# Down projection of a gated FFN: rounds 1 and 2 as seven block products instead of eight, with block sums on GpSimd

## What is computed

```
h2 = rmsnorm(x, norm2_g)
up, new_conv_f = causal_dwconv(h2 @ w_up, state_ffn_conv, conv_f_w, conv_f_b)   # 1024 -> 6144
gf, vf = split(up, 2)
x = x + (gelu(gf) * vf) @ w_down                                                # 3072 -> 1024
```

## Time and profile before

| | us |
|---|---|
| median of 3 runs | 1171.17 |
| lowest, highest | 1170.28, 1171.51 |
| span of the profiled execution, first to last instruction | 1168.8 |
| its own time | not listed apart from the span |
| PE busy | 1161.8 (99%) |
| DVE, ACT, POOL busy | 655.9 (56%), 455.9 (39%), 167.4 (14%) |

### The profile page before, as it was taken

The page is one execution under the profiler, slowest core; times in us unless marked ns, Lnnn a source line. Parts: engine busy times, 40 slices in busy tenths (PEclk is TensorE's granted clock), DMA queues, the critical chain, the costliest instruction groups (busy, mean ns, idle before and its releaser), DMA issues.

```text
span 1168.8 us, 21548 instructions
## 1 busy us (share of the span) xinstructions
PE 1161.8 (99%) x8959; PEld 1131.1 (97%) x8959; DVE 655.9 (56%) x1336; ACT 455.9 (39%) x719; POOL 167.4 (14%) x261
## 2 busy tenths in 40 slices
PE   8999999999999999999999999999999999999998
PEld 6999999999999999999999999999999999999998
DVE  7553544624522365756545559878347884378741
ACT  7444444434423367676443443222212222122221
POOL 2374153252330000000100120000000000000000
PEclk9999999999999999999999999999999999999999
DMA  8476255354431222221353223232322323232332
GB/s 242 144 212 174 79 140 150 97 149 124 132 93 55 73 77 74 85 73 56 123 143 90 73 73 90 72 90 77 91 80 83 88 73 95 72 90 72 90 99 61
DMA packets 183492, 118.50 MB, mean 101 GB/s; under 512 B 7114, under 2 KB 175694, under 8 KB 183418
## 3 DMA queue, kind: packets, MB, share of 16 engines
q1 hardware_dynamic: 172272, 89.44, 27.0%
q0 software_dynamic: 11056, 28.01, 8.6%
q10 hardware_dynamic: 90, 0.04, 0.0%
HBM read 107.43 MB, written 8.45 MB: 99 GB/s over the span
## 4 chain that ended last, share of the span: by engine, by line
PE 98%; DMA 1%; DVE 0%; ACT 0%; SPq 0%; issue 0%
PE ps L664 66%; PE ps L643 20%; PE ps L968 2%; PE ps L733 1%; PE ps L720 1%; PE ps L883 1%; PE ps L776 1%; PE ps L801 1%; PE ps L797 1%; PE ps L745 1%; PE ps L807 1%; DMA w_raw<-in_w_in 1%; PE ps L761 1%; PE ps L764 1%; PE ps L765 0%; PE ps L955 0%
## 5 line engine op out<-in xcount | busy, mean ns | idle before, releaser
L664 PE MATMUL ps<-h,w_s 128*128 128x288 f32 x3840 | 517.5, 296 | 0.0
L664 PEld LDWEIGHTS ps<-h,w_s 128*128 128x128 f32 x3840 | 512.6, 189 | 3.9 <-issue 3.9
L1453 DVE TENSOR_TENSOR w_s<-w_raw,w_s 128x1024 fp32r<-128x1024 f32 (+1 forms) x160 | 194.0, 1212 | 220.4 <-ACT w_s L1054 220.3
L1054 ACT ACTIVATE w_s<-w_raw 128x1024 fp32r<-128x1024 f32 (+1 forms) x160 | 166.3, 1039 | 334.4 <-PE ps L664 329.8
L643 PE MATMUL ps<-w_s,h 128*128 128x384 f32 x1152 | 217.5, 341 | 1.7 <-DVE w_s L1459 0.7
L643 PEld LDWEIGHTS ps<-w_s,h 128*128 128x128 f32 x1152 | 198.7, 188 | 3.7 <-DVE h L1480 1.2
L664 PE MATMUL ps<-g_hi,w_s 128*128 128x288 f32 x672 | 119.1, 297 | 0.0
L664 PEld LDWEIGHTS ps<-g_hi,w_s 128*128 128x128 f32 x672 | 99.4, 189 | 0.0
L664 PE MATMUL ps<-g_lo,w_s 128*128 128x288 f32 x336 | 71.9, 296 | 0.0
L605 POOL DMA_DIRECT2D out<-f_row x6 | 3.4, 567 | 415.1 <-ACT f_row L1403 415.1
L664 PEld LDWEIGHTS ps<-g_lo,w_s 128*128 128x128 f32 x336 | 54.1, 189 | 0.0
(11 more groups left out here) (309 smaller groups left out, 1429.3 us busy)
## 6 DMA issues: line engine op xcount, KB each, us to landing
w_raw<-in_w_in SPq DMA_DIRECT2D x65, 512.0 KB, 3.9
w_raw<-in_w_up SPq DMA_DIRECT2D x48, 512.0 KB, 3.9
w_raw<-in_w_down SPq DMA_DIRECT2D x24, 512.0 KB, 3.8
kc<-in_cache_k_g POOLq DMA_DIRECT2D x48, 128.0 KB, 3.2
vc<-in_cache_v_g POOLq DMA_DIRECT2D x12, 512.0 KB, 6.3
w_raw<-in_w_out SPq DMA_DIRECT2D x8, 512.0 KB, 3.8
w_raw<-in_w_br_a SPq DMA_DIRECT2D x7, 512.0 KB, 3.9
x_tok<-in_x_prompt SPq DMA_DIRECT2D x4, 512.0 KB, 8.3
```

What stands on the lines that cost most here:

```text
L664: last = mm(pu[u % 2][:, 512 * a:512 * a + HALF], w[:, part, k, :], x[:, k, HALF * a:HALF * (a + 1)], start=(k == 0 and i == 0), stop=(k = ...
L1054: A(w_s[:, ring(u), 0, 0:nkt[u], :], w_raw[:, u % NRAW, 0:nkt[u], :], ACT.Copy).then_inc(hi_ready, 1)
L1453: TT(w_s[:, ring(u), 1, 0:nkt[u], :], w_raw[:, u % NRAW, 0:nkt[u], :], w_s[:, ring(u), 0, 0:nkt[u], :], ALU.subtract).then_inc(lo_ready, 1)
```

## The change

In rounds 1 and 2 two down units (256 output columns) are taken together. The product of a 2 x 2 block matrix (output halves: the units x and y; contraction halves: k tiles 0 to 3 and 4 to 7) with a 2 x 2 block matrix of features (contraction halves; token halves of 288) is formed with seven block products in place of eight, by the Winograd form of Strassen's method. Each product is 4 k tiles of three matmuls, 12 in all. It needs:

- four sums of weight blocks per pair of units (`sums`, 512 columns each), on GpSimd (`left_sums`);
- sums of feature blocks, on GpSimd (`right_sums`): one of 288 columns in the first four pairs of a round, three in the last four; and their splits by ACT (`right_hi`, `right_sums_hi`) and DVE (`right_lo`, `right_sums_lo`), in the middle of the next pair;
- splits of seven weight blocks of 512 columns instead of two units of 1024, on ACT (`block_hi`) and DVE (`block_lo`), for the next pair of units beside the products of this one; the first pair of a round is split during pair 8 (or 16);
- products that share sums in PSUM: bank B starts as a copy of bank A after product 1, and bank C as a copy of B after product 3, both copies by ACT (`seed`); for the very first pair two matmuls write B and C once;
- five additions into `x2` per pair of units, by DVE (`taken_out`).

The state transposes come after the round's last product and wait for all additions; their taps move from DVE to ACT (`state_taps`, the same four copies). GpSimd stores the state rows after its sums. In the FFN the raw weights have a fourth buffer. Round 3 is as before, with one set of `g_hi` and `g_lo`. In the diff, which is cut to its core, BANK_A and BANK_G are the halves of `ps[2]`, BANK_B and BANK_C those of `ps[3]`; NSEV = 2 rounds, PRS = HK = 4; `block_at(s, n)` is the count of split blocks up to block n of pair s, and `st_hi`, `st_lo`, `st_sum`, `st_done`, `st_cp`, `st_ev` count high parts, low parts, sums, products, bank copies and additions.

```diff
+FIRST_ORDER, NEXT_ORDER = (3, 4, 1, 2, 5, 6, 7), (1, 2, 3, 4, 5, 6, 7)
+def block_order(s):
+    return NEXT_ORDER if s % PRS else FIRST_ORDER
+def block_at(s, n):
+    return 7 * s + block_order(s).index(n) + 1
+BLOCK_SLOT = {1: 0, 2: 1, 3: 4, 4: 5, 5: 6, 6: 2, 7: 3}
...
+        BANK_A, BANK_G, BANK_B, BANK_C = (ps[2 + q // 2][:, 512 * (q % 2):512 * (q % 2) + HALF] for q in range(4))
+        PRODUCT_BANK = {1: BANK_A, 2: BANK_G, 3: BANK_B, 4: BANK_A, 5: BANK_C, 6: BANK_B, 7: BANK_C}
+        PRODUCT_RIGHT = {1: b11, 2: t23[:, 1], 3: t23[:, 0], 4: b2x[:, 0], 5: t1x, 6: t4x, 7: b2x[:, 1]}
...
+        def left_source(s, n):
+            x, y = raw(pair_unit(s, 0)), raw(pair_unit(s, 1))
+            return {1: x[:, 0:HK, :], 2: sums[:, 1], 3: sums[:, 2], 4: x[:, HK:KT, :],
+                    5: sums[:, 0], 6: y[:, HK:KT, :], 7: sums[:, 3]}[n]
...
+                v = raw_before(u)
+                if v is None:
+                    sp.wait_ge(x2_ps, KT)
+                elif pair_of(v):
+                    s, half = pair_of(v)
+                    sp.wait_ge(st_sum, 4 * s + 4)
+                    sp.wait_ge(st_lo, block_at(s, 6) if half else max(block_at(s, 1), block_at(s, 4)))
+                else:
+                    sp.wait_ge(lo_ready, parts(v))
...
+            def left_sums(s):
+                x, y = raw(pair_unit(s, 0)), raw(pair_unit(s, 1))
+                raw_landed(pool, pair_unit(s, 0))
+                raw_landed(pool, pair_unit(s, 1))
+                if s:
+                    pool.wait_ge(st_sum, 4 * s)
+                    pool.wait_ge(st_lo, block_at(s - 1, 5))
+                pool.tensor_tensor(sums[:, 0], y[:, 0:HK, :], y[:, HK:KT, :], ALU.add).then_inc(st_sum, 1)
+                if s:
+                    pool.wait_ge(st_lo, block_at(s - 1, 2))
+                pool.tensor_tensor(sums[:, 1], x[:, 0:HK, :], y[:, 0:HK, :], ALU.subtract).then_inc(st_sum, 1)
+                pool.wait_ge(st_sum, 4 * s + 1)
+                if s:
+                    pool.wait_ge(st_lo, block_at(s - 1, 3))
+                pool.tensor_tensor(sums[:, 2], sums[:, 0], x[:, 0:HK, :], ALU.subtract).then_inc(st_sum, 1)
+                pool.wait_ge(st_sum, 4 * s + 3)
+                if s:
+                    pool.wait_ge(st_lo, block_at(s - 1, 7))
+                pool.tensor_tensor(sums[:, 3], x[:, HK:KT, :], sums[:, 2], ALU.subtract).then_inc(st_sum, 1)
+            def right_sums(i):
+                r, q = divmod(i, PPR)
+                j, n = q % HK, 16 * r
+                h0, h1 = slice(0, HALF), slice(HALF, TOK)
+                pool.wait_ge(gm_rdy, i + 1)
+                if q < HK:
+                    if i:
+                        pool.wait_ge(gs_lo, right_at(r, 5, j - 1) if q else 20 * r)
+                    pool.tensor_tensor(t_sum[:, :], gmr[:, j, h1], gmr[:, j, h0], ALU.subtract).then_inc(tt_rdy, 1)
+                    return
+                n += HK + 3 * j
+                pool.wait_ge(tt_rdy, n)
+                pool.tensor_tensor(gmr[:, j, h1], gm[:, h1], gmr[:, j, h1], ALU.subtract).then_inc(tt_rdy, 1)
+                pool.wait_ge(tt_rdy, n + 1)
+                pool.wait_ge(gs_lo, right_at(r, 1, j))
+                pool.tensor_tensor(gmr[:, j, h0], gmr[:, j, h1], gmr[:, j, h0], ALU.add).then_inc(tt_rdy, 1)
+                pool.wait_ge(tt_rdy, n + 2)
+                pool.wait_ge(gs_lo, right_at(r, 6, j - 1) if j else right_at(r, 5, HK - 1))
+                pool.tensor_tensor(t_sum[:, :], gm[:, h0], gmr[:, j, h0], ALU.subtract).then_inc(tt_rdy, 1)
+            for r in range(NSEV):
+                for q in range(1 if r else 0, PPR):
+                    right_sums(r * PPR + q)
+                    if q >= PPR - 2:
+                        left_sums(r * PRS + q - (PPR - 2))
+                if r + 1 < NSEV:
+                    right_sums((r + 1) * PPR)
+                for p in range(2, PRS):
+                    left_sums(r * PRS + p)
+                store_rows(r)
...
+            def seven(s):
+                r, first = s // PRS, s % PRS == 0
+                for n in range(1, 8):
+                    pe.wait_ge(st_lo, block_at(s, n))
+                    if n == 1 and s:
+                        pe.wait_ge(st_ev, 5 * (s - 1) + 2)
+                        if first:
+                            pe.wait_ge(frow_rdy, r)
+                    if n == 2 and s:
+                        pe.wait_ge(st_ev, 5 * (s - 1) + 1)
+                    if n in (3, 4):
+                        pe.wait_ge(st_cp, 2 * s + 1)
+                    if n == 5:
+                        pe.wait_ge(st_cp, 2 * s + 2)
+                    if n == 7:
+                        pe.wait_ge(st_ev, 5 * s + 3)
+                    w, x, bank = left_block(n), PRODUCT_RIGHT[n], PRODUCT_BANK[n]
+                    for k in range(HK):
+                        if first:
+                            pe.wait_ge(gs_lo, right_at(r, n, k))
+                        if s == 0 and n == 1 and k == 0:
+                            for seeded in (BANK_B, BANK_C):
+                                mm(seeded, w[:, 0, 0, :], x[:, 0, 0, :], start=True, stop=True)
+                        for i, (wp, xp) in enumerate(((0, 0), (0, 1), (1, 0))):
+                            last = mm(bank, w[:, wp, k, :], x[:, xp, k, :], start=(n < 3 and k == 0 and i == 0),
+                                      stop=(n in (2, 4, 6, 7) and k == HK - 1 and i == 2), skip_group_check=True)
+                    last.then_inc(st_done, 1)
...
                 pe.wait_ge(fst_rdy, (r + 1) * PPR)
+                if r < NSEV:
+                    pe.wait_ge(st_ev, 5 * PRS * (r + 1))
...
                 pairs(r * PPR + 1, min(PPR, NPAIR - 1 - r * PPR))
-                if r < NRND - 1:
-                    down(r, 0)
+                if r < NSEV:
+                    for p in range(PRS):
+                        seven(r * PRS + p)
                     state_rows(r)
-                    down(r, 1)
-                    with pe.Fori(0, KT // 2 - 1) as i:
-                        for j in range(2):
-                            u = down_unit(r, 2) + j
-                            looped_unit(u, PPR, i * 2 + parts(u), i + freed(u), g_hi[r % 2], g_lo[r % 2])
...
+            def right_sums_hi(i):
+                r, q = divmod(i, PPR)
+                if r >= NSEV or q < HK:
+                    return
+                j = q - HK
+                act.wait_ge(tt_rdy, 16 * r + HK + 3 * j + 2)
+                A(t23[:, :, 0, j, :], halves(gmr[:, j, :]), ACT.Copy).then_inc(gs_hi, 1)
+                act.wait_ge(tt_rdy, 16 * r + HK + 3 * j + 3)
+                A(t4x[:, 0, j, :], t_sum[:, :], ACT.Copy).then_inc(gs_hi, 1)
+            def block_hi(s, n):
+                first, bridge = s % PRS == 0, up_unit(PPR * (s // PRS + 1))
+                if n in (1, 4):
+                    raw_landed(act, pair_unit(s, 0))
+                elif n == 6:
+                    raw_landed(act, pair_unit(s, 1))
+                else:
+                    act.wait_ge(st_sum, 4 * s + {5: 1, 2: 2, 3: 3, 7: 4}[n])
+                if first and n in (1, 2, 6, 7):
+                    done(act, bridge + (n >= 6))
+                elif s:
+                    act.wait_ge(st_done, 7 * (s - 1) + n)
+                else:
+                    done(act, bridge - 1)
+                A(left_block(n)[:, 0], left_source(s, n), ACT.Copy).then_inc(st_hi, 1)
+            def seed(s, q):
+                act.wait_ge(st_done, 7 * s + (3 if q else 1))
+                if s:
+                    act.wait_ge(st_ev, 5 * (s - 1) + (5 if q else 4))
+                A(BANK_C if q else BANK_B, BANK_B if q else BANK_A, ACT.Copy).then_inc(st_cp, 1)
+            def state_taps(i):
+                act.wait_ge(cv_rdy, i + 1)
+                q = i % PPR
+                if q == 0 and i:
+                    act.wait_ge(fst_ps, i // PPR)
+                for j, b in enumerate((ug, uv)):
+                    x = b[:, i % 2, :]
+                    st = f_st[:, 2 * j + q % 2, :, q // 2]
+                    A(st[:, 0:2], x[:, US0 - 2:US0], ACT.Copy)
+                    last = A(seqs(st[:, 2:18], 2), seqs(x[:, US0:UW], USEQ)[:, :, USEQ - 2:USEQ], ACT.Copy)
+                last.then_inc(fst_rdy, 1)
...
+            def seven_hi(r, i):
+                for p in range(PRS):
+                    s, more = r * PRS + p, p + 1 < PRS
+                    seed(s, 0)
+                    if more:
+                        block_hi(s + 1, 1)
+                        block_hi(s + 1, 2)
+                    else:
+                        hi_split(up_unit(i + 1))
+                    seed(s, 1)
+                    if more:
+                        for n in range(3, 8):
+                            block_hi(s + 1, n)
+                    else:
+                        hi_split(up_unit(i + 1) + 1)
+                right_hi(i)
+                frows(r)
+                state_taps(i)
...
             for kind, i, m in ffn_steps():
```

(119 more changed lines are left out.)

143 lines of the change are left out of this document (98 added, 45 removed).

## The result

| | before | after |
|---|---|---|
| median us | 1170.72 (4 runs, 1169.6 to 1171.51) | 1182.25 (4 runs, 1181.73 to 1182.49) |
| ratio | | 1.0101, 95% interval 1.0086 to 1.0115 |
| span of the profiled execution | 1168.8 | 1180.7 |
| PE busy | 1161.8 | 1157.5 |
| mean granted clock | 1.000 | 0.994 |

The account below looks back on a forecast made before the run. PE was taken to bound the kernel. Per round 8.0 + 0.3 + 0.7 = 9.0 us lost, twice 18.0, less 12.53 gained, gives +5.5 on 1171.17: 1176.7; own range 1174.0 to 1182.4, 8-in-10 range 1164.8 to 1182.4.

Parts of the forecast that it names:

- PE work removed: Eight pairs of units take 84 matmuls instead of 96 each, less two seeding matmuls: 12.53 us gained.
- End of a round: State transposes now wait for the last addition into x2: 0.7 us lost per round.
- Steady pairs: Down pairs after the first: product 7's bank is tight in the second pair, 0.3 us (0 to 0.6); hidden from the third.
- The row that speaks against the change: Before the change, DVE steps with two SBUF inputs stood still until GpSimd's sum ended, twice out of two.
- Pair 7: GpSimd's first-pair sums beside DVE's up-pair steps: 1.5 us late if DVE goes first; taken as nearer that, 2.0.
- GpSimd first: Bound where GpSimd wins when both queues are ready: pair 7 3.8 us late, PE waiting 0.7 for pair 8's weights.
- The bridge: Pair 8 (and 16) into the first down products: product 7 6.0 us late, 2.4 if GpSimd holds nothing; 8.0 with pair 7.
- The clock: Rival, chance 0.05: PE stands 2 to 4 us at each bridge, the clock falls, 2.9 us lost twice: 1182.5 us.
- The rival where the sums hide: Chance 0.25: GpSimd's sums fall into DVE's waits, the bridge costs DVE's own 2.4 and transposes 0.7: 1164.8 us.
- Half hidden: Rival, chance 0.11: GpSimd holds DVE only where it began first, DVE catches up at its waits: 1170.4 us.
- the lower pace: Rival, chance 0.05: waits inside the first pair's products or a lower matmul pace give back more: 1179 us.

Follow-up runs that it names:

- a1: Changed kernel with every GpSimd sum of weight blocks cut from 512 to 32 columns per partition, waits and orders kept; 1163.78 us.
- a2: Changed kernel with GpSimd's weight sums cut to 32 columns per partition for the first pair of each round only; 1174.30 us.
- a4: Changed kernel with 38 unread matmuls added per round, before the waits of products 1 and 7 of a round's first pair; 1179.37 us.
- b3: Changed kernel, sums still on GpSimd; pair 8's convolution, gelu and product moved behind later down products, second and third additions before splits of blocks 2 to 4; 1169.83 us.
- c1: Changed kernel, all sums on GpSimd, with convolution deferred, additions first, and bridge blocks 3, 4, 1, 2 split before pair 7's right sums; 1166.41 us.

## Why the prediction failed

The direction was right, the size was not: 5.5 us were forecast, 11.5 measured. The sum was 2 x (8.0 + 0.3 + 0.7) lost; measured are 13.5 and 11.1.

- **PE work removed, 12.53.** Right: the pace in one bank is 0.133, and the shift between the spans adds up with it.
- **End of a round, 0.7.** Right: 0.8 in both rounds.
- **Steady pairs, 0.3.** There was no wait at all in the second pair, nor later.
- **The row that speaks against the change.** Right, and the largest part (a1). It was too narrow: DVE's one-input convolution step (1.54) and a copy of 16 columns between SBUF buffers (0.79 at 795.53 and at 957.03, otherwise 0.17), the latter beside a sum of features, are held as well, which left fewer steps that can lie beside a sum. By the Trainium skill (SBUF — State Buffer, "Who interferes with whom") copies and `tensor_scalar` can take the shared pair too, in modes that use both ports; the 1.54 us of that step agree.
- **Pair 7, "nearer DVE first: 2.0".** Wrong. The queues take turns, GpSimd is held only for the rest of one DVE step and DVE for nearly a whole sum each time. Four steps lost 4.2 us, over my "GpSimd first" bound of 3.8, and PE waited 2.0 for pair 8's weights, where I had 0.7 at that bound and nothing in the sum. Of the 4.2 only 2.6 reached PE (a2), so that the 2.0 in the sum was 0.6 short.
- **The bridge.** 8.0 forecast for pair 7 and bridge together; the waits at products 1, 5 and 7 and before pair 8 come to 8.45 and 8.65. Product 3 was not late in the changed kernel, because product 1 was so late itself. The parts were right too: 6.0 for the bridge by itself, 5.8 and 6.1 in a2; 2.4 of it DVE's own queue, 2.1 and 2.4 in a1. Only the lower end of the range doesn't follow from its working, which gives 6.0 for the bridge and then uses 5.5; with 6.0 it is 1175.0.
- **The clock, the term that is missing.** I made it a rival with a chance of 0.05, "PE would stand 2 to 4 us", and left it out of the sum. It cost 4.3 us in round 1 and 1.7 in round 2, 6.0 of the 6.6 by which the loss was forecast too small (24.6 against 18.0). The rival's price was two falls of 2.9; there were three, of 1.5, 2.8 and 1.7, with nearly the same sum. The step that failed was to argue for stops of that length and then to count on the clock through them. The Trainium skill (TensorE: Matmul & The Clock Gate, "HAM oscillation") has a kernel whose matmuls start slow behind each wait of some 3 to 5 us. The trace agrees, with slow products behind stops and a4's fast ones where the stop was filled, but here shorter stops were enough: 2.3 us before product 1, 1.8 in a4.

Two numbers agree with the 1182.25 by luck. The upper end of the range, 1182.4, stands for 10.6 us of waits at pair 7 and the bridge with the clock kept, where there were 8.45 and 8.65; and the clock rival's 1182.5 has two falls of 2.9.

The rival where the sums hide fell in this kernel. Its price (1164.8) is that of a1, where they are nearly gone. "Half hidden" fell as well, since DVE did not catch up (it is busy all through both stops), and so did the lower pace: 46 products run at 1.60.

## What to carry to other kernels

A sum of SBUF data moved to GpSimd isn't beside DVE's steps on SBUF data but in turns with them (1.0 to 1.1 us for each sum of 1.28): charge its whole duration to DVE in every stage where DVE has less room than that. Moving work off the path was worth more here than moving it to another engine: with all sums left on GpSimd the order gave 12.4 us (b3) and 15.8 (c1), and the engine 4.6 to 5.9 more. When your own sum makes PE stand for some 2 us, put the slow matmuls behind it into the sum.
